# Order of small work on VectorE and ScalarE in a mixer, a chain in two steps, and two last sums

## What is computed

```python
# layer 1
a = rmsnorm(h, norm1[i]);  proj = a @ w_in[i]
u, qf, kf, vf, fl, qs, ks_, vs = jnp.split(proj, IN_SPLITS, axis=-1)
y_pool = multiscale_pool_mixer(u, pool_w[i], pool_scale[i])
y_fox = head_rmsnorm(forgetting_attention(qf, kf, vf, log_sigmoid(fl + bias)), fox_out_gain[i])   # 6 heads
y_sb = head_rmsnorm(stick_breaking_attention(qs, ks_, vs), sb_out_gain[i])                        # 6 heads
h = h + jnp.concatenate([y_pool, y_fox, y_sb], axis=-1) @ w_out[i]
h = h + (silu(a @ w_gate[i]) * (a @ w_up[i])) @ w_down[i]       # a = rmsnorm(h, norm2[i])
# layer 2
h = rmsnorm(h, final_norm);  p = rms_norm(h, norm1_g) @ w_in_2
y = concatenate([rwkv7_time_mix(p_rwkv), nsa_attention(p_nsa)])
h = h + y @ w_out_2
h = h + swiglu(rms_norm(h, norm2_g), w_gate_2, w_up_2, w_down_2)
return rms_norm(h, norm_f_g)
# stick breaking: a row of weights is exp(log_beta + sum of log(1 - beta) over the keys between)
# rwkv7, for each head and token: sa = S a_t;  S = S * w_t + sa b_t' + v_t k_t';  y_t = S r_t
```

## Time and profile before

| | us |
|---|---|
| median of three runs | 769.67 (769.62 to 771.64) |
| the profiled execution | 772.29 |
| its span in the trace | 770.5 |
| PE busy | 737.6 |
| DVE busy | 504.5 |
| ACT busy | 419.1 |
| mean granted clock of PE | 0.986 of full |

### The profile page before, as it was taken

One profiled execution on the slowest core, in us unless ns is written; L12 is line 12 of the kernel. 1 busy time (PEld: TensorE's weight loads), 2 busy tenths in 40 slices (PEclk: granted clock), 3 DMA queues, 4 the chain that ended last, 5 costly groups with the idle time before them and its releaser, 6 DMA issues.

```text
span 770.5 us, 16318 instructions
## 1 busy us (share of the span) xinstructions
PE 737.6 (96%) x6562; PEld 664.4 (86%) x6562; DVE 504.5 (65%) x910; ACT 419.1 (54%) x742; POOL 5.6 (1%) x13
## 2 busy tenths in 40 slices
PE   6999998999999999998999999989999999999996
PEld 5777776998888899996999998888898888889996
DVE  4554556668999994346567875444569999995443
ACT  5545544565666663337786662333467666665331
POOL 0000000000000000001000000000000000000000
PEclk9989999999999999999999999999999999999998
DMA  6613333236765555542343332301145555555531
GB/s 226 223 56 110 110 110 110 100 120 219 268 239 178 206 176 192 189 166 107 111 165 110 110 110 111 113 3 58 56 165 178 205 193 188 182 199 174 202 115 55
DMA packets 16738, 113.78 MB, mean 148 GB/s; under 512 B 2000, under 2 KB 2128, under 8 KB 3632
## 3 DMA queue, kind: packets, MB, share of 16 engines
q1 hardware_dynamic: 15984, 109.22, 39.8%
q0 software_dynamic: 704, 3.85, 1.4%
HBM read 112.01 MB, written 1.05 MB: 147 GB/s over the span
## 4 chain that ended last, share of the span: by engine, by line
PE 86%; ACT 5%; DVE 5%; issue 2%; DMA 1%; SPq 0%; DVEq 0%; ACTq 0%
PE ps L573 21%; PE ps L558 12%; PE ps L560 11%; PE ps L559 11%; PE ps L575 11%; PE ps L910 5%; PE ps L992 2%; ACT w_hi L1391 1%; DVE w_lo L1871 1%; PE ps L1048 1%; PE ps L872 1%; DMA ring<-in_weights 1%; PE ps L977 1%; DMA vec<-in_vecs 1%; PE ps L950 0%
## 5 line engine op out<-in xcount | busy, mean ns | idle before, releaser
L1871 DVE TENSOR_TENSOR w_lo<-ring,w_hi 128x1024 fp32r<-128x1024 f32 x194 | 237.2, 1223 | 133.1 <-ACT w_hi L1391 131.7
L1391 ACT ACTIVATE w_hi<-ring 128x1024 fp32r<-128x1024 f32 x194 | 204.0, 1054 | 104.4 <-PE ps L560 90.5
L573 PE MATMUL ps<-acts,w_hi 128*128 128x512 f32 x704 | 246.4, 393 | 0.0
L575 PE MATMUL ps<-acts,w_lo 128*128 128x256 f32 x704 | 197.4, 280 | 0.0
L573 PEld LDWEIGHTS ps<-acts,w_hi 128*128 128x128 f32 x704 | 132.2, 188 | 29.9 <-issue 0.4
L558 PE MATMUL ps<-acts,w_hi 128*128 128x256 f32 (+1 forms) x464 | 139.9, 302 | 6.9 <-DVE acts L1879 2.9
L560 PE MATMUL ps<-acts,w_lo 128*128 128x256 f32 (+1 forms) x464 | 133.0, 287 | 0.0
L559 PE MATMUL ps<-acts,w_hi 128*128 128x256 f32 (+1 forms) x464 | 132.8, 286 | 0.0
L575 PEld LDWEIGHTS ps<-acts,w_lo 128*128 128x128 f32 x704 | 132.3, 188 | 0.1
L558 PEld LDWEIGHTS ps<-acts,w_hi 128*128 128x128 f32 x464 | 89.1, 192 | 14.2 <-issue 7.5
L560 PE MATMUL ps<-hid_hi,w_lo 128*128 (+1 forms) x352 | 99.6, 283 | 0.0
(11 more groups left out here) (363 smaller groups left out, 918.8 us busy)
## 6 DMA issues: line engine op xcount, KB each, us to landing
ring<-in_weights SPq DMA_DIRECT2D x101, 1024.0 KB, 4.8
res<-in_xT SPq DMA_DIRECT2D x2, 544.0 KB, 4.3
ring<-in_weights SPq DMA_DIRECT2D x2, 512.0 KB, 5.2
cst<-in_consts POOLq DMA_DIRECT2D x1, 1024.0 KB, 5.1
out_features<-yT SPq DMA_DIRECT2D x4, 256.0 KB, 2.0
cst<-in_consts POOLq DMA_DIRECT2D x1, 945.5 KB, 5.0
vec<-in_vecs POOLq DMA_DIRECT2D x1, 677.0 KB, 4.2
cst<-in_consts POOLq DMA_DIRECT2D x1, 656.0 KB, 5.2
```

The source lines that it names most:

```text
L573: pe.matmul(ps[:, bank, :].rearrange("p (x t) -> p x t", x=2), w_hi[:, slot, k, :], acts[:, :, at, 0:SEQ], start=(k == 0), stop=(k == KT - ...
L575: return pe.matmul(ps[:, bank, 0:SEQ], w_lo[:, slot, k, :], act_hi[:, at, 0:SEQ], start=False, stop=(k == KT - 1), skip_group_check=True)
L1391: act.activation(w_hi[:, t % SLOTS].rearrange("p k c -> p (k c)"), ring[:, b % RING, half].rearrange("p k c -> p (k c)"), ACT.Copy)\
L1871: dve.tensor_tensor(w_lo[:, t % SLOTS].rearrange("p k c -> p (k c)"), ring[:, b % RING, half].rearrange("p k c -> p (k c)"), w_hi[:, t % S ...
```

## The change

1. In the loop of mixer 1, DVE takes the mixer's pieces that are ready ahead of `split_lo`; `keep_sb` and `fox_maxima` stay behind it. ACT takes `fox_exps` and `sb_weights` ahead of `head_root`.
2. The last two down tiles of both layers are taken together, output tile by output tile: six products for f = 0, then six for f = 1, and so on. Output tile 7 gets bank 0 for itself. Four down tiles, not one, stand ahead of the loop, which then has four rounds of four. `add_down` is called for one tile at a time; the last two don't wait for their pair. At the border, the split of the fourth tile from the end of the ring's slots moves behind the down products, on ACT ahead of the plain squares.
3. RWKV: `w1t` and `a_tok` go, with two `turn_tokens`. For each chunk c > 0, `from_state(c)` multiplies a by the state, DVE adds the result to `kav` (`keep_taken`), and `sa_of(c)` multiplies T by the sum.
4. At the end, DVE adds the squares of tiles 1 to 5 to that of tile 0 (`gather_square`) between its down adds; PE sums three tiles instead of eight. DVE multiplies by the gain ahead of the root, and by the root in four instructions of two tiles.

```diff
@@ TensorE: down products
+                def out_place(f):
+                    return ps[:, 0, 0:SEQ] if f == KT - 1 else ps[:, 4 + f // 2, (f % 2) * SEQ:(f % 2 + 1) * SEQ]
+                def last_downs():
+                    for d in (FT - 2, FT - 1):
+                        pe.wait_ge(S("w_split"), t_down + d + 1)
+                        pe.wait_ge(S("hid_ready"), (layer - 1) * FT + d + 1)
+                    for f in range(KT):
+                        mm = part_products(out_place(f), (t_down + FT - 2) % SLOTS, f, hid_hi[:, FT - 2, :],
+                                           hid_lo[:, FT - 2, :], False, False)
+                        if f == KT - 1:
+                            mm.then_inc(S("down_used"), 1)
+                        part_products(out_place(f), (t_down + FT - 1) % SLOTS, f, hid_hi[:, FT - 1, :],
+                                      hid_lo[:, FT - 1, :], False, True).then_inc(S("down_ready"), 1)
-                down(0)
-                with pe.Fori(0, (FT - 2) // UNROLL) as i:
+                for d in range(UNROLL):
+                    down(d)
+                with pe.Fori(0, (FT - 2 - UNROLL) // UNROLL) as i:
                     for u in range(UNROLL):
-                        down(1 + u, i)
-                down(FT - 1)
+                        down(UNROLL + u, i)
+                last_downs()
@@ TensorE: RWKV chain
+            def from_state(c):
+                pe.wait_ge(S("state_grown"), c)
+                by_head((3, 6, 0)[c - 1], lambda c, j: chunk_of(ar[:, 0], c, j),
+                        lambda c, j, hs: states[hs, c - 1, j, :], (c,)).then_inc(S("taken_terms"), 1)
+            def sa_of(c):
+                if c > 0:
+                    pe.wait_ge(S("taken_kept"), c)
+                by_head((0, 4)[c // 2], lambda c, j: xt[:, c * PAIRS + j, :],
+                        lambda c, j, hs: kav[hs, c * PAIRS + j, :], (c,), (c % 2) * SEQ).then_inc(S("sa_terms"), 1)
...
-            own_sa(0)
-            own_sa(1).then_inc(S("sa_terms"), 1)
-            from_state(1, 2, 3)
+            sa_of(0)
             turn_tokens(2, key_raw, 1)
             cmp_turn()
-            pe.wait_ge(S("tokens_kept"), 9)
+            pe.wait_ge(S("tokens_kept"), 7)
             state_ahead(0)
-            pe.wait_ge(S("xt_grown_1"), LEVELS - 1)
-            own_sa(2)
-            own_sa(3)
-            from_state(2, 4, 6)
             state_after(0)
-            pe.wait_ge(S("tokens_kept"), 10)
+            pe.wait_ge(S("tokens_kept"), 8)
             cmp_values(2)
-            pe.wait_ge(S("w1_kept"), 1)
-            sa_of(1)
+            from_state(1)
             state_ahead(1)
+            sa_of(1)
+            pe.wait_ge(S("xt_grown_1"), LEVELS - 1)
             state_after(1)
             nsa_features(2)
-            pe.wait_ge(S("w1_kept"), 2)
-            sa_of(2)
+            from_state(2)
             state_ahead(2)
+            sa_of(2)
             outputs(0)
             state_after(2)
             pe.wait_ge(S("normed"), normed("mixer2", 3))
             out_part(2, 0, 0, 0)
-            sa_of(3)
+            from_state(3)
             out_part(2, 0, 0, 1)
+            sa_of(3)
@@ TensorE: last sums
-            sum_squares("norm6", SEQ)
+            for at, k in enumerate((0, KT - 2, KT - 1)):
+                if k == 0:
+                    pe.wait_ge(S("squares_gathered"), KT - 3)
+                else:
+                    pe.wait_ge(S("norm_squares"), (nth("norm6") - 1) * KT + k + 1)
@@ ScalarE
                 if at == 5 and 0 <= r < 3:
+                    fox_exps(r)
+                    sb_weights(r)
                     if r > 0:
                         head_root(r - 1)
-                    fox_exps(r)
-                    sb_weights(r)
...
+            split_hi(T_IN2 + SLOTS - 2)
             for k in range(5):
                 plain_square(k)
@@ VectorE: mixer 1
-                split_lo(T_IN1 + t + SLOTS)
...
                 if at == 1 and r > 1:
                     rest_heads(r - 2)
-                if at == 1 and 0 < r < 3:
-                    keep_sb(r - 1)
                 if at == 3 and 0 <= r < 3:
                     sb_negated_logs(r)
                     if r > 0:
                         keep_fox(r - 1)
                 if at == 4 and 0 <= r < 3:
                     sb_rests(r)
+                split_lo(T_IN1 + t + SLOTS)
+                if at == 1 and 0 < r < 3:
+                    keep_sb(r - 1)
+                if at == 4 and 0 <= r < 3:
                     fox_maxima(r)
@@ VectorE: RWKV
+            def keep_taken(c):
+                dve.wait_ge(S("taken_terms"), c)
+                n = slice(c * PAIRS, (c + 1) * PAIRS)
+                dve.tensor_tensor(kav[:, n, :].rearrange(flat3), ps[:, (3, 6, 0)[c - 1], 0:SEQ],
+                                  kav[:, n, :].rearrange(flat3), ALU.add).then_inc(S("taken_kept"), 1)
...
             split_lo(T_OUT2 + 1)
+            keep_taken(1)
             keep_sa(1)
@@ VectorE: end
+            for t in range(KT):
+                add_down(2, t)
+                if 1 <= t - 1 <= KT - 3:
+                    gather_square(t - 1)
+            for k in range(KT):
+                dve.wait_ge(S("down_added"), KT + k + 1)
+                dve.tensor_scalar(yT[:, k, :], res[:, k, META:CTX], V("norm6", k), None, ALU.mult)\
+                    .then_inc(S("gained"), 1)
             dve.wait_ge(S("norm_root"), nth("norm6"))
-            for k in range(KT):
-                dve.scalar_tensor_tensor(yT[:, k, :], res[:, k, META:CTX], V("norm6", k), nrm[:, 1, 0:SEQ],
-                                         ALU.mult, ALU.mult).then_inc(S("final_ready"), 1)
+            for k in range(0, KT, 2):
+                dve.wait_ge(S("gained"), k + 2)
+                dve.tensor_tensor(yT[:, k:k + 2, :], yT[:, k:k + 2, :],
+                                  nrm[:, 1, 0:SEQ].unsqueeze(1).to_broadcast([P, 2, SEQ]), ALU.mult)\
+                    .then_inc(S("final_ready"), 2)
```

More of the change, by code:

```diff
@@ L466, in down_ahead @@
         def down_ahead(layer):
-            return FT - 1 if layer == 1 else FT - SLOTS
+            return FT - 2 if layer == 1 else FT - SLOTS
         block = ctx.enter_context(nc.Block())
@@ L584, in have @@
                 pe.wait_ge(landed[b % RING], 16 * (b // RING + 1))
-            def sum_squares(name, tokens):
-                for k in range(KT):
-                    pe.wait_ge(S("norm_squares"), (nth(name) - 1) * KT + k + 1)
-                    mm = pe.matmul(ps[:, norm_bank(name), 0:tokens], C("ones"), sq[:, k, 0:tokens],
-                                   start=(k == 0), stop=(k == KT - 1))
-                mm.then_inc(S("norm_sums"), 1)
             def feed_forward(layer, t_up):
@@ L638, in down @@
                     pe.wait_ge(S("hid_ready"), step + ((layer - 1) * FT + d + 1))
-                    last = d == FT - 1
                     if i is None:
@@ L1086, in _ @@
             products(1)
-            turn_tokens(3, ar[:, 0], 0)
             pe.wait_ge(S("products_masked"), 1)
@@ L1237, in _ @@
             grow_xt(0, 4)
-            turn_tokens(2, ar[:, 0], 1)
             grow_xi(1, 4)
@@ L1250, in _ @@
             grow_xt(1, 5)
-            def own_sa(c):
-                return by_head((0, 4)[c // 2], lambda c, j: xt[:, c * PAIRS + j, :],
-                               lambda c, j, hs: kav[hs, c * PAIRS + j, :], (c,), (c % 2) * SEQ, start=(c != 3),
-                               stop=(c == 0))
-            def from_state(c0, c1, bank):
-                by_head(bank, lambda c, j: a_tok[:, c * PAIRS + j, :], lambda c, j, hs: xt[hs, c * PAIRS + j, :],
-                        range(c0, c1)).then_inc(S("w1_ready"), 1)
+            def from_state(c):
[7 more added lines that the diff above has]
+                        lambda c, j, hs: kav[hs, c * PAIRS + j, :], (c,), (c % 2) * SEQ).then_inc(S("sa_terms"), 1)
             def state_ahead(c):
@@ L1277, in state_after @@
                         (c % 2) * SEQ, start=False).then_inc(S("state_terms"), 1)
-            def sa_of(c):
-                pe.wait_ge(S("state_grown"), c)
-                by_head((0, 4)[c // 2], lambda c, j: w1t[:, (c - 1) * PAIRS + j, :],
-                        lambda c, j, hs: states[hs, c - 1, j, :], (c,), (c % 2) * SEQ, start=False)\
-                    .then_inc(S("sa_terms"), 1)
             def outputs(cp):
@@ L1354, in _ @@
             feed_forward(2, T_UP2)
-            sum_squares("norm6", SEQ)
+            for at, k in enumerate((0, KT - 2, KT - 1)):
[3 more added lines that the diff above has]
+                    pe.wait_ge(S("norm_squares"), (nth("norm6") - 1) * KT + k + 1)
+                mm = pe.matmul(ps[:, norm_bank("norm6"), 0:SEQ], C("ones"), sq[:, k, 0:SEQ], start=(at == 0),
+                               stop=(at == 2))
+            mm.then_inc(S("norm_sums"), 1)
         @block.scalar
@@ L1794, in _ @@
             keep_join(1, 3)
-            keep_tokens(4, 2, kav, 0)
+            keep_tokens(3, 2, kav, 0)
```

(12 more changed lines are left out.)

65 lines of the change are left out of this document (31 added, 34 removed).

## The result

| us | before | changed |
|---|---|---|
| median of the runs | 769.83 (769.62 to 771.64, 4) | 762.72 (760.67 to 763.83, 4) |
| the profiled execution | 772.29 | 760.67 |
| its span | 770.5 | 758.9 |

The ratio is 0.9899, with a 95% interval of 0.9874 to 0.9925: shorter by 7.1 us in the medians, clear of the noise, though only 1%. The forecast was 757.1 with a range of 754.0 to 761.0; the time lies outside, on the slow side.

The account below looks back on a forecast made before the run. PE was taken as the bound, busy 737.6 of 770.5 us. Mixer 1 8.0, border 1.2, RWKV 1.7 and tail 1.7 sum to 12.6; 769.67 - 12.6 = 757.1 us, range 754.0 to 761.0.

Parts of the forecast that it names:

- The base: Whole kernel: the sum of 12.6 us, made on the 772.29 us execution's trace, is taken off the median of 769.67.
- The clock term: Mixer 1, behind the first sums: low clock cost 2.5 us there; 1.8 of it counted as gain.
- the first gap: Mixer 1, PE's wait before the first sb_sums: 1.9 us goes, plus 1.8 for the clock, 3.7 in all.
- Mixer 1 without the clock: Mixer 1's forecast gain was 3.7 + 1.1 + 3.2 = 8.0 us, including 1.8 for the clock.
- The new wait of 1.4: End of mixer 1: PE waits 1.4 us for DVE's copy before fox_values(2), which still starts 3.2 sooner.
- Border: Border to layer 2: Ln and the first products come 1.2 us sooner, bounds 0.4 and 1.4.
- RWKV: RWKV stage: two turns removed give 1.9 us, chain net 0, stall takes 0.2: gain 1.7, bounds -1.1 and +4.3.
- The stall: RWKV stage, PE's wait without releaser: late instructions, 1.8 us after instead of 1.7, bounds 0.3 and 3.7.
- Tail: Kernel's end, last product to end: 8.5 us instead of 10.2, gain 1.7, bounds 0.7 and 1.9.
- (F): RWKV stage: after a stall of 1.8 us or more the clock falls and stays low, up to 796 us; chance 0.04.
- (B): Clock falls in mixer 1's new wait or behind the RWKV stall, 1.8 us each: 758.9, both 760.7; chance 0.22.
- The low clock in the RWKV stage: RWKV stage: a low clock there was named as a sign that the prediction is wrong.

Follow-up runs that it names:

- e5: Kernel before with only parts 2 and 4 of the change: twelve executions, mean 769.1 us.
- e7: Kernel before with only ScalarE's (ACT's) half of part 1: one execution, 774.21 us.
- e1: Kernel before, unchanged, run again: 11 executions, median 770.07 us (768.6 to 776.9).
- e4: Kernel before with only part 3, the RWKV part of the change: twelve executions, mean 773.1 us.
- e14: Kernel before with only VectorE's (DVE's) half of part 1, repeated in six executions: mean 764.8 us.
- e3: Kernel before with only part 1, both VectorE's and ScalarE's order in mixer 1: six executions, mean 764.4 us.
- e6: Kernel before with only VectorE's (DVE's) half of part 1: one execution, 757.83 us.
- e2: Changed kernel, unchanged, run again: 5 executions, median 761.23 us (758.53 to 764.40).
- e12: Changed kernel with earlier keep_sb(2), gelu first, twelve down tiles ahead of the loop, from_state(3) before the first output part: six executions, mean 756.1 us, ratio 0.9796.

## Why the prediction was wrong, point by point

**The base.** "I make the sum on the trace and take it off the median." This is the step that failed, and no bound or rival of the range allowed for it. The profiled execution of 772.29 was the usual one and the median of 769.67 came from quick ones; the median of 73 is 772.44. The sum taken off that gives 759.8, which is 1.9 to 2.7 from what the changed kernel does (mean 761.76, median 762.52), and the range moved by the same 2.8 is 756.8 to 763.8, with the measured 762.72 inside. I saw the difference of 2.6 between profile and median and put it down to a rare fall of the clock in the profile, while the list of low stretches in one trace was all I had. One trace says where the clock was low once, not how often.

**The clock term, 1.8.** Counted as if the fall at 45 us went and nothing came for it. It does go: the low stretch of 6.8 us behind the first gap stands in three of the five profiles that have the gap (before, e5, e7; not e1 and e4), and in none of the eleven without it. But the clock falls at other places, in the changed kernel as in the kernel before. The measured saving is 1.3 +- 0.7.

**Mixer 1 without the clock, 6.2.** Right. From first product to last forget product before needed 126.09 in e1 with one low stretch at 22 to 25 us. The same stretch of the clock costs 2.2 to 2.5 (119.48 in e14 and 119.76 in e3, with it, against 117.30 in e6 without), so 123.7 at full clock, and 117.3 after: 6.4. The new wait of 1.4 was forecast to the tenth. Wrong in it were the credit to ScalarE's half, and the new wait as something new: it stood at 1.53 in e1.

**Border, 1.2.** Measured 1.47. Ln came 3.5 us after the last product's end (341.70 - 338.20) where I had 3.8.

**RWKV, 1.9 for the transposes and net 0 for the chain.** From the first product of the stage (450.22 in e6, 461.17 in e4) to the first output product, without the stall, it takes 75.89 us in e6 and 74.32 in e4: 1.57 of the 1.9, so the chain costs 0.3. Then 0.8 is given back among the output parts, which I had mentioned ("one group more stands between output parts") and then left at nothing. Net 0.8. In the sum itself the stall was named as 0.1 and taken as 0.2.

**The stall, -0.1.** The mechanism (late instructions) and the place (two groups before `cmp_folded`) were right, and 1.8 for the mean is what it is. The way there had a slip: half of 256 instructions are 64 products, 1.9 us, where I wrote 3.7. What the change costs here depends on what is taken for before: against the two profiles of the kernel before (mean 2.1) it gains 0.3, against all six with its code on TensorE (mean 1.1) it loses 0.7.

**Tail, 1.7.** Measured 1.6. I had missed a wait of 0.75 before the last sums (751.03) on the last gathered square, and was too careful elsewhere.

By rows, then: 6.4 + 1.5 + 0.8 + 1.6 = 10.3, and the stall, -0.7 or +0.3: 9.6 or 10.6, where the prediction had 10.8. The executions at equal clock say 9.3 +- 0.3, which is nearer to 9.6; I go on with that. So of the 5.6 us between 757.1 and 762.7, 2.8 are the base (772.44 - 769.67), 1.2 the sum by rows (1.6 in the RWKV stage and its stall, less 0.4 won elsewhere), 0.5 the clock term (1.8 - 1.3); that makes 761.6, and the remaining 1 is that the median of the changed kernel's four runs, 762.72, lies above its mean of 15, 761.76.

**Rivals.** (F) had a true half: the clock does fall in the RWKV stage. Its fatal half is refuted, since it rose again within the same 64x64 groups, after 3.4 us both times in the profile after. It costs 1.4 to 1.5 us for each stretch (491.38 to 494.66 takes 3.28 us here, the same three groups in before 504.24 to 506.12, 1.88). The low clock in the RWKV stage, which I had put down as a sign of being wrong, was no test of the change, as the kernel before shows it too (e1). (B) priced exactly such falls, but only behind the two waits that I knew; the low stretches at 71 to 75 and 105 to 109 us in e2 have no wait of PE's over 0.15 us in the 50 us ahead of the first (the last one is 1.80, at 20.94), so my rule of thumb, idle first and then the fall, is not enough to forecast one.

## What to carry to other kernels

Before a sum is taken off a median, ask how the executions spread and with what: here three runs said 769.6 to 771.6 and seventy-three said 768.3 to 778.9, most of it along the granted clock. Make the sum between stretches at full clock, take the base at the same clock, and give the clock a spread of its own instead of a term. And a group that is pushed between two streams of large matmuls costs more than its own length; put it into a wait, as e12 does.

## What the runs showed of the hardware

- The granted clock falls at different places in different executions of the same kernel, in stretches of 3.4 or 6.8 us at half speed. Between the execution with no such stretch before its tail (756.0 us span) and others of the same program (up to 764.7) lie 8.7 us.
- A stall of TensorE without a releaser comes back at one product of the program and differs in size: 1.40 to 2.65 us with the same kernel, and 0.57 to 2.49 with the same code on TensorE alone. Its place moves with the code, which fits steps of 256 instructions, and TensorE goes on 1.3 to 1.6 us behind the end of a 16 KB packet of instructions that came 5.5 to 8.1 us after the one before. The Trainium skill ("Runtime: NRT & Kernel Launch", Instruction fetch mechanics) has the crossing from one block of instructions to the next mostly hidden; the steps of 256 bear out the crossing, the 0.57 to 2.65 us that show bear against hidden. That the loads of the weights are what holds the instructions up was read from the DMA rows and not tried.
- Sixteen 64x64 products take 0.47 us from start to start among their like. Between 128-row products they take 0.61, and 0.8 with the longer steps at both borders.
